# A four-part change in a long transformer kernel: expert picking, one-hot rows, cross attention and modulation loads

## What is computed

```python
q = einsum('td,dhk->thk', x_t, w_q).reshape(T, 8, 2, 128)
s = einsum('thpk,hpnk->thpn', q, sub_keys)          # 128 keys, two halves, 8 heads
sv, si = lax.top_k(s, 16)
cand = sv[:, :, 0, :, None] + sv[:, :, 1, None, :]  # 16 x 16 sums
fv, fpos = lax.top_k(cand, 16)
gate = softmax(fv)                                  # of 16384 experts, 16 per head and token
act = gelu(einsum('thkd,td->thk', u_emb[eidx], x_t))
y = einsum('thk,thkd->td', gate * act, v_emb[eidx])
```

## Time and profile before

| | |
|---|---|
| median of 3 runs | 2669.27 us (2668.14 to 2672.26) |
| profiled execution | 2670.9 us, its span 2669.1 us |
| PE busy | 2458.3 us, 92% |
| DVE busy | 1829.0 us, 69% |
| ACT busy | 1308.6 us, 49% |
| POOL busy | 509.7 us, 19% |
| mean granted TensorE clock | 0.963 |
| moved by DMA | 480.58 MB, 180 GB/s on average |

### The profile page before, as it was taken

The page is one execution under the profiler, slowest core; times in us unless marked ns, Lnnn a source line. Parts: engine busy times, 40 slices in busy tenths (PEclk is TensorE's granted clock), DMA queues, the critical chain, the costliest instruction groups (busy, mean ns, idle before and its releaser), DMA issues. The chain is left out here.

```text
span 2669.1 us, 46969 instructions
## 1 busy us (share of the span) xinstructions
PE 2458.3 (92%) x17864; PEld 2244.9 (84%) x17864; DVE 1829.0 (69%) x3756; ACT 1308.6 (49%) x1990; POOL 509.7 (19%) x328
## 2 busy tenths in 40 slices
PE   5698999998999999778999999999999987887998
PEld 4588999997887888668999998788887966886998
DVE  5675888858777776772888866766666556554754
ACT  3345665546544455454665456555555534044443
POOL 0000766623000000200476763000000020000000
PEclk8799999999999999879999999999999998999999
DMA  8755777782788886724777773477774532042554
GB/s 350 270 168 151 182 182 182 182 268 31 250 260 257 264 259 196 263 95 129 181 185 182 181 182 94 146 215 219 215 219 138 188 130 72 18 134 72 169 167 153
DMA packets 200516, 480.58 MB, mean 180 GB/s; under 512 B 54448, under 2 KB 87728, under 8 KB 199760
## 3 DMA queue, kind: packets, MB, share of 16 engines
q1 hardware_dynamic: 150960, 431.75, 51.9%
q10 hardware_dynamic: 12576, 47.29, 4.9%
q0 software_dynamic: 36864, 0.15, 3.6%
HBM read 461.15 MB, written 17.96 MB: 179 GB/s over the span
## 5 line engine op out<-in xcount | busy, mean ns | idle before, releaser
L278 DVE TENSOR_TENSOR weight_low<-weight_raw,weight_high 128x1024 fp32r<-128x1024 f32 x732 | 892.9, 1222 | 423.3 <-ACT weight_high L272 418.3
L272 ACT ACTIVATE weight_high<-weight_raw 128x1024 fp32r<-128x1024 f32 x732 | 773.9, 1059 | 698.7 <-DMA weight_raw<-peer_v_dram 340.7
L382 PE MATMUL bank<-h_high,weight_high 128*128 128x256 f32 x3424 | 984.1, 287 | 72.6 <-DVE h_low L537 21.7
L382 PE MATMUL bank<-h_low,weight_high 128*128 128x256 f32 x3424 | 980.5, 286 | 0.0
L382 PE MATMUL bank<-h_high,weight_low 128*128 128x256 f32 x3424 | 980.1, 286 | 0.0
L382 PEld LDWEIGHTS bank<-h_high,weight_high 128*128 128x128 f32 x3424 | 669.9, 196 | 84.6 <-issue 75.2
L382 PEld LDWEIGHTS bank<-h_low,weight_high 128*128 128x128 f32 x3424 | 669.9, 196 | 0.0
L382 PEld LDWEIGHTS bank<-h_high,weight_low 128*128 128x128 f32 x3424 | 669.3, 195 | 0.0
L1171 POOL DMA_INDIRECT gate_table<-pick_expo,pick_spot x256 | 466.6, 1823 | 683.3 <-DVE pick_expo L1273 398.2
L1452 PE MATMUL bank<-weight_high,act_high 128*128 128x512 f32 x1024 | 317.6, 392 | 7.9 <-DVE act_low L1519 6.1
L1452 PE MATMUL bank<-weight_low,act_high 128*128 128x512 f32 x1024 | 316.8, 391 | 0.0
(11 more groups left out here) (348 smaller groups left out, 2560.3 us busy)
## 6 DMA issues: line engine op xcount, KB each, us to landing
weight_raw<-peer_u_dram SPq DMA_DIRECT2D x256, 512.0 KB
weight_raw<-peer_v_dram SPq DMA_DIRECT2D x256, 512.0 KB
kept<-ada_later_dram ACTq DMA_DIRECT2D x54, 512.0 KB, 4.7
gate_table<-kept ACTq DMA_DIRECT2D x8, 2048.0 KB, 18.3
weight_raw<-peer_w_q_dram SPq DMA_DIRECT2D x32, 512.0 KB
kept<-gate_table SPq DMA_DIRECT2D x256, 64.0 KB, 3.5
weight_raw<-w_in_dram SPq DMA_DIRECT2D x32, 512.0 KB
weight_raw<-mlp_w_up_dram SPq DMA_DIRECT2D x32, 512.0 KB
```

What stands on the lines that cost most here:

```text
L272: self.nc.scalar.activation(self.high[:, slot, :], self.raw[:, slot, :], ACT.Identity) \
L278: eng.tensor_tensor(self.low[:, slot, :], self.raw[:, slot, :], self.high[:, slot, :].bitcast(F32), ALU.subtract) \
L382: mm = self.nc.tensor.matmul(out, w, x, start=(start and i == 0), stop=(stop and i == 2), skip_group_check=skip)
```

## The change

1. `setup` issues two of the four 2 MB modulation loads; the other two (blocks 24 to 31) are issued by the projection's stream behind tiles 5 and 7, whose loop is written out.
2. `peer_queries`' second block picks head 0 of the first token half on VectorE, ahead of the three low halves. `peer_scores` picks the other 15, spread over the same tiles, with `picked_at` shifted by one head, and GpSimd scatters all eight heads there.
3. `peer_weigh`: the second one-hot rows of groups 3, 7, 11, ... are made by GpSimd, with a semaphore of their own.
4. `cross_attention`: the block of transposes is merged into the attention block, in banks 6 and 7, copied by ScalarE behind the first exponentials. Scores of two heads are made at the start, and VectorE's peaks of head h + 2 stand behind the weights of head h; ScalarE's exponentials of head h + 1 stand ahead of the copies of head h.

```diff
@@ Core.stream
+    def stream(self, sp, seg, k, behind=None):
+        if behind is not None:
+            for n in range(RING, seg.count):
+                self.load_tile(sp, seg, n, n % RING)
+                if n in behind:
+                    behind[n](sp)
@@ setup
-            for q in range(4):
+            for q in range(2):
                 load_modulations(core, sp, q)
@@ even_mixer
+                behind={5: lambda sp: load_modulations(core, sp, 2), 7: lambda sp: load_modulations(core, sp, 3)})
@@ peer_queries
         def _(dve):
+            link = Chain(step, dve)
+            dve.wait_ge(cleared.sem, 16 * CLEARINGS * (layer + 1))
+            dve.wait_ge(kept.sem, kept.at(1))
+            for _ in pick_experts(core, link, scores, 0, 0):
+                pass
             core.first_parts(dve, "lows")
@@ picked_at
-    return max(RING - 1, ((h + 1) * PICK_STEPS - 1) * PICKED_BY // (TT * HEADS * PICK_STEPS) + 1)
+    return max(RING - 1, (h * PICK_STEPS - 1) * PICKED_BY // ((TT * HEADS - 1) * PICK_STEPS) + 1)
@@ peer_scores
-            scatter_gates(core, pool, layer, range(SCATTERED_EARLY))
+            scatter_gates(core, pool, layer, range(HEADS))
...
-            done, all_steps = 0, TT * HEADS * PICK_STEPS
+            done, all_steps = 0, (TT * HEADS - 1) * PICK_STEPS
@@ peer_weigh
         def _(pool):
-            scatter_gates(core, pool, layer, range(SCATTERED_EARLY, HEADS))
+            for g in range(ring - 1, groups, ring):
+                onehots(nc.gpsimd, pool, g).then_inc(fourths.sem, 1)
...
             for g in range(0, groups, 2):
-                if g + 2 < groups:
-                    onehots(g + 2)
-                    onehots(g + 3)
+                for ahead in (g + 2, g + 3):
+                    if ahead < groups and ahead % ring != ring - 1:
+                        onehots(nc.vector, dve, ahead).then_inc(seconds.sem, 1)
                 multiply(g)
@@ cross_attention, TensorE
             scores(0)
+            scores(1)
+            for n, (t, d) in enumerate(quarters):
+                if n >= 2:
+                    pe.wait_ge(turned_kept.sem, turned_kept.at(n - 1))
+                transposes(core, pe, [kv[:, 8 + d + i, t * P:(t + 1) * P] for i in range(4)], [core.bank[6 + n % 2]], turned)
...
+                if h + 2 < 4:
+                    scores(h + 2)
@@ cross_attention, VectorE
+            peaks(0)
+            peaks(1)
             for h in range(4):
...
                 j.then_inc(weighed.sem, 1)
+                if h + 2 < 4:
+                    dve.wait_ge(weighed.sem, weighed.at(h + 1))
+                    peaks(h + 2)
@@ cross_attention, ScalarE
+            exponentials(0)
+            keep_turned(0)
+            keep_turned(1)
+            for h in range(4):
+                if h + 1 < 4:
+                    exponentials(h + 1)
+                if h < 1:
+                    keep_turned(2)
+                    keep_turned(3)
...
+                if h >= 1:
+                    take_mixed(h - 1)
+            take_mixed(3)
```

More of the change, by code:

```diff
@@ L254, in first_tiles @@
                 self.load_tile(sp, self.segments[k], slot, slot)
-    def stream(self, sp, seg, k):
-        if seg.count > RING:
+    def stream(self, sp, seg, k, behind=None):
[4 more added lines that the diff above has]
+                    behind[n](sp)
+        elif seg.count > RING:
             with sp.Fori(1, seg.count // RING) as g:
@@ L383, in product, with linear @@
         return mm
-    def linear(self, engine, take, groups=1, rhs=None, loads=(), aside=None, per_tile=1, norm=None, squares=None, root=None, aside_act=None, issue=None, halves=None, first=None):
+    def linear(self, engine, take, groups=1, rhs=None, loads=(), aside=None, per_tile=1, norm=None, squares=None, root=None, aside_act=None, issue=None, halves=None, first=None, behind=None):
         nc, sig = self.nc, self.sig
@@ L402, in _ @@
                     sp.dma_start(dst, self.dram[name]).then_inc(loaded.sem, 16)
-                self.stream(sp, seg, k)
+                self.stream(sp, seg, k, behind)
                 if loads:
@@ L1043, in peer_queries @@
         core.linear("scalar", core.copy_to(queries), loads=loads, norm=ffn_norm(core, layer))
-    scored, kept = sig("keys_scored"), sig("key_scores_kept")
+    scored, kept, step, cleared = sig("keys_scored"), sig("key_scores_kept"), sig("dve_step"), sig("table_cleared")
+    scores = core.arena[:, SCORES_AT:SCORES_AT + 4096].rearrange("p (t h s n) -> p t h s n", t=TT, h=HEADS, s=2)
     with nc.Block() as block:
@@ L1069, in _ @@
         def _(dve):
+            link = Chain(step, dve)
[3 more added lines that the diff above has]
+                pass
+            step.used = link.n
             core.first_parts(dve, "lows")
+    step.close(step.used)
     scored.close(8)
@@ L1257, in _ @@
             link = Chain(step, dve)
-            picking = (i for t in range(TT) for h in range(HEADS) for i in pick_experts(core, link, scores, t, h))
+            picking = (i for t in range(TT) for h in range(HEADS) if t + h for i in pick_experts(core, link, scores, t, h))
             steps = modulations(core, dve, range(EARLY_MODS, EARLY_MODS + IN_KEYS))
-            done, all_steps = 0, TT * HEADS * PICK_STEPS
+            done, all_steps = 0, (TT * HEADS - 1) * PICK_STEPS
             dve.wait_ge(cleared.sem, 16 * CLEARINGS * (layer + 1))
@@ L1309, in peer_weigh, with onehots @@
     iota, eye, minus_iota = core.c("iota"), b.spread_by[:, 0, :], b.spread_by[:, 1, :]
+    fourths = sig("fourth_seconds_ready")
+    def onehots(engine, eng, g):
+        if g >= ring:
+            eng.wait_ge(spread.sem, spread.at(g - ring + 1))
+        for u in range(4):
+            token = 4 * g + u
+            i = engine.tensor_scalar(group(hot_second, g)[:, u, :], iota, second[:, token:token + 1],
+                                     gate[:, token:token + 1], ALU.is_equal, ALU.mult)
+        return i
     with nc.Block() as block:
@@ L1375, in _ @@
         def _(dve):
-            def onehots(g):
-                if g >= ring:
-                    dve.wait_ge(spread.sem, spread.at(g - ring + 1))
-                for u in range(4):
-                    token = 4 * g + u
-                    i = nc.vector.tensor_scalar(group(hot_second, g)[:, u, :], iota, second[:, token:token + 1],
-                                                gate[:, token:token + 1], ALU.is_equal, ALU.mult)
-                i.then_inc(seconds.sem, 1)
             def multiply(g):
@@ L1403, in peer_weigh @@
     gated.close(HEADS + 1)
-    for s in (seconds, firsts, spread, taken, differ, distant):
+    seconds.close(groups - groups // ring)
+    fourths.close(groups // ring)
+    for s in (firsts, spread, taken, differ, distant):
         s.close(groups)
@@ new lines, in exponentials @@
+            def exponentials(h):
+                mine = small[:, 8 * (h % 2):8 * (h % 2) + 8]
+                act.wait_ge(peaked.sem, peaked.at(h + 1))
+                if h >= 2:
+                    act.wait_ge(flipped.sem, flipped.at(h - 1))
+                for i in range(2):
+                    j = nc.scalar.activation(probs[:, 2 * (h % 2) + i, :], core.bank[h % 2][:, i * T:(i + 1) * T], ACT.Exp,
+                                             bias=mine[:, 2 + i:3 + i], scale=scale, accum_out=mine[:, 4 + i:5 + i])
+                j.then_inc(exped.sem, 1)
@@ L2644, in cross_attention @@
+            take_mixed(3)
+    turned.close(4)
+    turned_kept.close(4)
     step.close(step.used)
```

61 lines of the change are left out of this document (31 added, 30 removed).

## The result

The changed kernel takes 2654.7 us (median of 5 runs, 2649.49 to 2669.42) where the kernel before, run beside it on the same chip, took 2669.81 (2668.14 to 2674.28). The ratio is 0.9946, 95% interval 0.9923 to 0.997: some 14 us less. The forecast was 2663.3, range 2653 to 2677. The direction was right and the time lies in the range, but not in the 2659 to 2667 that the forecast gave for itself; the size was that of rival (a), no collision in Part 3, to within a microsecond (2655.3).

A forecast was written before the change was run, and what follows sets the result against it. TensorE was taken to bound the kernel, the change moving only four stretches where it waits. Terms -2.9 + 3.1 - 3.0 - 3.2 = -6.0 us took the median 2669.27 to 2663.3, range 2653 to 2677.

The forecast's parts named there:

- rival (a): Gate stage: no collision, VectorE's freed time all gained, 11 us; sum -14.0, so 2655.3 us; chance 0.2.
- Part 3: Gate stage: GpSimd making every fourth group's one-hots relieves VectorE but collides with it; 1.5 us a layer, 3 saved in all.
- Part 1: Input projection: moving two loads lands tile 4 sooner, with new waits at tiles 6 and 8; 2.9 us earlier.
- rival (c): Start and cross attention: clock dips take the small gains, eighth head's scatter outlasting its block included; +0.6, 2670 us; chance 0.2.
- Part 2: Key scores: low halves queue behind the first head's pick, costing 3.1 us over both layers; earlier scatters of eight heads stay hidden.
- The 4 to 5 us for not starting earlier: Block of the scores: cost of GpSimd's eighth head if its scatters did not start earlier, 4 to 5 us.
- the two engines collide: Gate stage: a VectorE one-hot started within GpSimd's waits for its end, losing about 0.3 us; 0.6 to 1.2 a period.
- my own formula (four hits of 0.7): Gate stage: GpSimd one-hots at 0.91 us with four hits make the period 5.4 + 4 x 0.7 = 8.2, 15 us lost a layer.
- The bound on that side: Gate stage without collisions: four groups cost VectorE 5.4 us instead of 6.36, gaining 5.5 us a layer at best.
- Part 4: Cross attention: reordered transposes and scores end it 3.6 us sooner, 1.8 of it the lower clock; taken as 3.2.
- my bound of 4.5: Cross attention: upper bound on the gain from the new order, 4.5 us, the lower being 1.4.
- Rival (b): Gate stage: GpSimd's one-hot takes 0.7 us and three of four hit VectorE, 8.8 us lost; sum +5.8, 2675 us; chance 0.21.

The follow-up runs named there:

- after_again: The changed kernel unedited, run again for a second trace: 2658.07 us, ratio 0.9944 to the kernel before.
- gpsimd_beside: Changed kernel with all one-hot rows made by VectorE, while GpSimd makes 52 unread one-hot rows a layer; layer 0's gate stage took 56.2 us.
- gpsimd_products: Changed kernel with all one-hot rows made by VectorE, while GpSimd makes 100 unread two-tensor products; layer 0's gate stage took 64.3 us.
- after: The changed kernel's first measurement and trace: median 2654.7 us, profiled execution 2669.42 us.
- forms: Changed kernel plus unread VectorE test operations at each gate stage's start, GpSimd resting, making one-hots or products; eight 128-column one-hots: 3.02, 3.06, 3.25 us.

## Why the prediction came out as it did

**Part 1** was right in mechanism and, in the first pair of traces, in size: -3.0 against -2.9, with the landings within 0.5 us. Over more traces it is less: the last eviction lies at 84.4 to 85.6, mean 85.1, in the four that load all blocks first, and at 81.8 to 84.4, mean 83.0, in the eight with the two behind tiles 5 and 7, so 2.1 us. The dips of rival (c) do occur, and cost less than it said. In after_again the clock fell behind the wait for tile 6 (window, columns as above; the clock is 0.67):

```profile
64.00:68.00 4.00, 4.00 (x26) 4.00 (x25) 1.69 (x3) 0.36 (x1) 0.00 (x0) 0.67 1.03 410
```

Yet its projection ends at 81.8, as early as any: the slower tiles used up the wait for tile 8, which is not in its timeline.

**Part 2** was right: +1.4 and +1.9, sum 3.3 against 3.1; by the means over traces (three before: 17.8 and 17.3; nine: 19.0 and 18.9) it is 2.9. That the earlier start of the scatters pays for eight heads was right as well in layer 1, from whose rows I had it; in layer 0, for which the forecast has no sum, it is barely so. The 4 to 5 us for not starting earlier hold for a layer (4.8 and 5.8), not for both.

**Part 3** is where the forecast missed: -9.3 in the first traces (4.1 and 5.2) and 10.7 in the medians, against -3.0. Over all traces of a kind the stage takes 54.2 and 54.7 us before (three) and 49.0 in either layer with GpSimd's share (seven): 10.9. The step that failed is "the two engines collide: VectorE's addition of two SBUF tensors takes 1.05 us while GpSimd multiplies, 0.69 when it has stopped". The row was read rightly and carried over to another pair of forms. This is what GpSimd did beside that addition of the earlier trace rows (`tensor_tensor`, as is the addition), in the trace of before:

```profile
1098.03 12.56 POOL L1745 TENSOR_TENSOR arena<-arena,trig 128x512 f32<-128x512 f32 x8
```

Both engines read two tensors there. The one-hots of both engines read one tensor and two pointers. gpsimd_beside puts the price of GpSimd's being busy all the time at 0.11 us in 3.18, where I took 0.6 to 1.2 in 5.4; gpsimd_products shows that beside GpSimd's two-tensor form the same one-hots would have lost 0.17 us each. A second error did no harm, which was luck: GpSimd's one-hot takes 0.85 us, not 0.5, near the upper bound of 0.91. By my own formula (four hits of 0.7) that alone would have meant nearly 15 us lost a layer. It cost nothing, since four of them, 3.41, still fit into a period of 5.48, and in neither layer's stage did TensorE wait for GpSimd's one-hots.

The bound on that side, 5.4 us a period and 5.5 a layer, was right: 5.48, and 5.2 and 5.7 by the means. Its arithmetic was looser than its result: 6.36 less 5.4, times 8, is 7.7, not the "6 to 7" from which I took one. TensorE needs 5.36 for the same four groups, so by this estimate a larger share for GpSimd would bring some 0.1 us a period at most; no run tried it.

The rule of the Trainium skill, "SBUF — State Buffer", section "Who interferes with whom", that whoever starts first has the shared ports for the whole instruction and the other blocks, and that a tensor_scalar of VectorE may be one of those, was the argument against this part. Where GpSimd makes products, gpsimd_products agrees: VectorE's one-hots go in step with them at 0.43 us. Where GpSimd makes one-hots, gpsimd_beside doesn't: 0.014 us each. The measurement decides. What in GpSimd's instruction makes the difference, no run here shows.

**Part 4** was right in mechanism and low in size: -3.2 against -3.6 (upper clock before) to -5.2 (lower). Of the forecast's 3.6, 1.8 was the clock, so the new order itself was put at 1.8 us and is worth 3.6, and the 5.2 of the first pair lie above my bound of 4.5. I had also taken off 0.4 for a clock dip that never came in the new order. The rest is spread over the heads. In the first trace the first mix ends 9.85 us after the first scores, where I had 10.7, and the ends of the mixes follow each other by 4.17, 3.39 and 3.12 us, where I had 4.6, 3.4 and 3.4. For the last head the weights are ready 2.2 us before the mix ahead of it ends, so only the transposes of the weights, their copy and the mix are left in the chain.

**The sum.** With the terms of the first traces: -3.0 + 3.3 - 9.3 - 5.2 = -14.2; with the mean of Part 1 (-2.1) and the upper clock in the old attention (-3.6) it is -11.7; with the means over all traces of a kind for every part (-2.1, +2.9, -10.9, and -4.1 for the attention, whose three traces before have a mean of 25.5) it is -14.2. The medians say -15.1 on the first chip and -16.6 on the second. The undone parts, as differences of medians to after_again, are 1.0, 10.7 and 4.8 for Parts 1, 3 and 4; these three undos leave Part 2 in, with its cost of 3.3, so they should exceed the whole by that, and they sum to 16.5, not to 19.9. The 3 us between are within what medians with intervals of 0.2% can say. Rival (a) came true, at a chance of 0.2; that the range holds the result is owed to that rival, which had stretched it down to 2653, and not to my own sum of -6.0. Rival (b) fell: with GpSimd's one-hots even slower than it says, none of VectorE's took 0.5 us (0.47 at most in the first trace). Rival (c) fell as a whole: its dips belong to single executions and did not take the gains. What it has with them, that the eighth head's scatter outlasts its block, did happen in layer 0 of one trace, gpsimd_beside.

## What to carry to other kernels

A collision between VectorE and GpSimd is priced for a pair of forms. Take it from a row in which both engines run the forms in question; where there is none, give the case of no collision a fair chance as well; here it was the truth. Before a piece of work is given to a slow engine, compare its whole time with the period (3.41 in 5.48), not its time per operation with that of the fast one. And read a change of 0.5% by stages over several traces: one stretch without an edit lies anywhere from 347.7 to 359.9 us in kernels of one kind, and a lower clock in another costs 2.5 to 2.9.

## What the runs showed of the hardware

- GpSimd's one-hot of 128 columns takes 0.82 to 0.85 us back to back (gpsimd_beside, after), its product of two tensors of 128 columns 0.41 to 0.45 (gpsimd_products, forms). The form with one tensor is the slower one and disturbs VectorE less.
- VectorE's one-hots of 128 columns without waits between them: 0.26 us each with GpSimd at rest, 0.27 beside its one-hots, 0.43 beside its products. With a wait after each: 0.38, 0.38 and 0.41, so the waits hide most of it. Copies of 256 columns, with a wait after each, go from 0.32 to 0.40 beside GpSimd's one-hots and 0.46 beside its products.
- The granted clock at the same place of the same program (layer 0's query projection) was in 161 to 165 us 1.00 in one execution and 0.50, the level of 1.2 GHz, in two. It had fallen in all three, behind an idle time of TensorE of 1.8 to 2.3 us, and stayed down for 3.4 us in the one and 10.2 in the two, which are 2.5 and 2.9 us longer over that stretch.
